# Loads of a kernel's opening in another order, and one modulation tile moved from VectorE to TensorE

## The reference

```python
def ada_mods(cvec, w, b):
    m = jax.nn.silu(cvec) @ w + b
    return [t[:, None, :] for t in jnp.split(m, 6, axis=-1)]

def post_norm_layer(x, mods, mixer, channel, ln):
    sh1, sc1, g1, sh2, sc2, g2 = mods
    y, state = mixer(x * (1 + sc1) + sh1)
    x = layer_norm(ALPHA * x + g1 * y, ln[0], ln[1])
    x = layer_norm(ALPHA * x + g2 * channel(x * (1 + sc2) + sh2), ln[2], ln[3])
    return x, state
```

## Time and profile before

| | |
|---|---|
| median of 3 runs | 1607.42 us (1606.74 to 1607.65) |
| the profiled execution | 1608.91 us |
| its span, first to last instruction | 1607.2 us |
| TensorE busy | 1505.2 us, 94% of the span |
| VectorE busy | 1262.9 us, 79% |
| ScalarE busy | 798.8 us, 50% |
| GpSimd busy | 333.4 us, 21% |
| mean granted clock of TensorE | 0.973 |
| mean DMA rate | 218 GB/s |

### The profile page before, as it was taken

The page is one execution under the profiler, slowest core; times in us unless marked ns, Lnnn a source line. Parts: engine busy times, 40 slices in busy tenths (PEclk is TensorE's granted clock), DMA queues, the critical chain, the costliest instruction groups (busy, mean ns, idle before and its releaser), DMA issues. The chain is left out here.

```text
span 1607.2 us, 23836 instructions
## 1 busy us (share of the span) xinstructions
PE 1505.2 (94%) x8787; PEld 1362.6 (85%) x8787; DVE 1262.9 (79%) x1667; ACT 798.8 (50%) x1066; POOL 333.4 (21%) x410
## 2 busy tenths in 40 slices
PE   5999999799999998999999797899999999999996
PEld 1768876599999998997776695899999999999994
DVE  6868798688887977987778644788888888888884
ACT  1222222533332226545677325567677776777763
POOL 1201003600101103004995043001011010110104
PEclk9999999899999999999998899999999999999998
DMA  9534344256566632323221036689999999999960
GB/s 384 196 104 162 128 144 144 104 209 222 212 225 229 229 117 88 131 106 118 80 82 63 0 141 255 252 301 370 369 377 356 348 365 364 382 351 347 364 245 40
DMA packets 50151, 349.68 MB, mean 218 GB/s; under 512 B 6016, under 2 KB 6416, under 8 KB 22432
## 3 DMA queue, kind: packets, MB, share of 16 engines
q1 hardware_dynamic: 31392, 278.88, 45.0%
q0 software_dynamic: 18256, 68.30, 12.9%
q10 hardware_dynamic: 432, 1.57, 0.2%
HBM read 335.22 MB, written 13.50 MB: 217 GB/s over the span
## 5 line engine op out<-in xcount | busy, mean ns | idle before, releaser
L1992 DVE TENSOR_TENSOR arena_r<-arena,arena_r 128x2816 fp32r<-128x2816 f32 x132 | 406.1, 3090 | 54.4 <-ACT arena_r L1117 53.0
L2862 PE MATMUL ps<-arena_r,uT_r 128*128 128x352 f32 (+1 forms) x1188 | 367.1, 309 | 0.0
L1117 ACT ACTIVATE arena_r<-arena 128x2816 fp32r<-128x2816 f32 x132 | 337.4, 2556 | 54.2 <-PE ps L2862 52.1
L2862 PE MATMUL ps<-arena_r,zT_r 128*128 128x352 f32 x1408 | 346.7, 327 | 5.7 <-DVE uT_r L2090 4.3
L2498 PE MATMUL ps<-sqT_r,arena_r 128*128 128x384 f32 x963 | 260.2, 342 | 7.5 <-DVE uT_r L1658 7.5
L2862 PEld LDWEIGHTS ps<-arena_r,zT_r 128*128 128x128 f32 x1408 | 247.3, 189 | 6.1 <-DVE arena_r L1992 6.1
L2862 PEld LDWEIGHTS ps<-arena_r,uT_r 128*128 128x128 f32 x1188 | 224.9, 189 | 0.0
L2498 PEld LDWEIGHTS ps<-sqT_r,arena_r 128*128 128x128 f32 x963 | 178.1, 190 | 8.5 <-issue 8.5
L2862 PE MATMUL ps<-arena_r,spare_r 128*128 128x256 f32 x968 | 177.8, 285 | 4.0 <-DVE arena_r L1992 4.0
L2498 PE MATMUL ps<-arena_r,arena_r 128*128 128x384 f32 x848 | 160.7, 342 | 8.3 <-DVE arena_r L1862 5.7
L2498 PEld LDWEIGHTS ps<-arena_r,arena_r 128*128 128x128 f32 x848 | 149.9, 191 | 11.2 <-DVE arena_r L1862 6.5
(11 more groups left out here) (459 smaller groups left out, 2481.6 us busy)
## 6 DMA issues: line engine op xcount, KB each, us to landing
arena<-in_w_moe SPq DMA_DIRECT2D x132, 1408.0 KB, 7.6
arena<-in_w_up SPq DMA_DIRECT2D x22, 1024.0 KB, 4.9
zT<-in_w_adav POOLq DMA_DIRECT2D x32, 512.0 KB, 4.8
arena<-in_w_xbc SPq DMA_DIRECT2D x12, 1024.0 KB, 4.9
arena<-in_w_down SPq DMA_DIRECT2D x8, 1408.0 KB, 6.4
spare<-in_w_adav POOLq DMA_DIRECT2D x20, 512.0 KB, 5.2
sqT<-in_w_adav POOLq DMA_DIRECT2D x16, 512.0 KB, 3.9
arena<-in_w_z SPq DMA_DIRECT2D x8, 1024.0 KB, 4.8
```

Of the source, the lines that this page charges most:

```text
L1117: nc.scalar.activation(whi[s % PAIRS], slot(s % MRING), ACT.Copy) \
L1992: V.tensor_tensor(wlo[s % PAIRS], slot(s % MRING), whi[s % PAIRS].bitcast(F32), ALU.subtract) \
L2862: m = M.matmul(out, a, b, start=first and n == 0, stop=last and n == 2)
```

## The change

`ADA_PE` goes from 4 to 5 and `ADA_FIRST` from 4 to 3: one of the eight first tiles moves from VectorE, and from GpSimd's queue, to TensorE and SyncE's queue. The fifth tile uses slot 0 again, so its load waits for the first tile's matmuls. All later tiles move one slot on in the ring.

On SyncE's queue the order becomes `cvec`, tile 0, `consts`, tile 1, `pvec`, tiles 2, 3 and 4, `xT`, `masks`. The condition now counts on `x_in`: ScalarE's first SiLU waits for the condition alone, and `modulate` for the condition, `xT` and the masks. `ada_turn` waits for the constants and column vectors at its first call.

On VectorE `ada_first`, `modulations` and `modulate` come ahead of the mask cast, `sel2` and the identity cast.

```diff
--- before.py
+++ after.py
@@ -67,7 +67,7 @@
 NPV = _at
 
 
-ADA, ADA_PE, ADA_FIRST = 24, 4, 4
+ADA, ADA_PE, ADA_FIRST = 24, 5, 3
 ADA_UP, ADA_TURN = 32, (0, 2, 3, 1)
 ADA_REST = 2 * (ADA - ADA_PE - ADA_FIRST)
 
@@ -468,10 +468,7 @@
 
         @block.sync
         def _(sp):
-            sp.dma_start(cons[:, :], i["consts"]).then_inc(S("consts_in"), 16)
-            sp.dma_start(pvec[:, :], i["pvec"]).then_inc(S("consts_in"), 16)
-            sp.dma_start(masks, i["masks"]).then_inc(S("consts_in"), 16)
-            sp.dma_start(cvec, i["cvec"]).then_inc(S("consts_in"), 16)
+            sp.dma_start(cvec, i["cvec"]).then_inc(S("x_in"), 16)
 
             def load(name, width, t, k):
                 g = FIRST[name] + t
@@ -486,6 +483,10 @@
                     if first + t >= RING:
                         sp.wait_ge(*tile_done(first + t - RING))
                     load(name, width, t, t)
+                    if (name, t) == ("ada0a", 0):
+                        sp.dma_start(cons[:, :], i["consts"]).then_inc(S("consts_in"), 16)
+                    elif (name, t) == ("ada0a", 1):
+                        sp.dma_start(pvec[:, :], i["pvec"]).then_inc(S("consts_in"), 16)
                 loops = (n - head) // RING
                 if loops:
                     with sp.Fori(0, loops) as it:
@@ -500,7 +501,9 @@
             for name, *_ in STAGES:
                 stream(name)
                 if name == "ada0a":
+                    sp.wait_ge(S("x_in"), 16)
                     sp.dma_start(xT[:, :, :], i["xT"]).then_inc(S("x_in"), 16)
+                    sp.dma_start(masks, i["masks"]).then_inc(S("x_in"), 16)
 
             def load_expert(e, s):
                 sp.dma_start(slot(s % MRING), i["w_moe"][e, s] if isinstance(e, int) else
@@ -758,7 +761,7 @@
                                              bias=mod(layer, 3 * half, b, grp), scale=mod(layer, 3 * half + 1, b, grp))
                 k.then_inc(S("u_ready"), 1)
 
-            act.wait_ge(S("consts_in"), 64)
+            act.wait_ge(S("x_in"), 16)
             nc.scalar.activation(cact, cvec, ACT.Silu).then_inc(S("cact_ready"), 1)
             act.wait_ge(S("cond_in"), 16)
             nc.scalar.activation(crow[0], crow[0], ACT.Silu).then_inc(S("cond_ready"), 1)
@@ -1374,19 +1377,18 @@
             step(V.memset(onesf[:, :], 1.0))
             step(V.memset(epsc, EPS))
             step(V.memset(onesm[:, :], 1.0 / D))
-            v.wait_ge(S("consts_in"), 64)
+            v.wait_ge(S("cond_ready"), 1)
+            ada_first()
+            v.wait_ge(S("consts_in"), 32)
+            v.wait_ge(S("tr_mm"), ADA_PE)
+            modulations(0, 0, 2 * KB, 1)
+            v.wait_ge(S("x_in"), 48)
+            modulate(0, 0, 0)
             step(V.tensor_copy(maskb16[:, :, :], masks))
             twins = ident.rearrange("p (e w h) -> p e w h", e=2, w=2)
             step(V.tensor_tensor(sel2[:, :].rearrange("p (e h) -> p e h", e=2), twins[:, :, 0, :], twins[:, :, 1, :],
                                  ALU.add))
             step.done(V.tensor_copy(identb16[:, :], ident), S("b16_ready"), 1)
-
-            v.wait_ge(S("cond_ready"), 1)
-            ada_first()
-            v.wait_ge(S("tr_mm"), ADA_PE)
-            modulations(0, 0, 2 * KB, 1)
-            v.wait_ge(S("x_in"), 16)
-            modulate(0, 0, 0)
             step(V.memset(vaug[:, :, :, HD:VA], 1.0))
             ada_rest(4)
 
@@ -2187,6 +2189,8 @@
             def ada_turn(t):
 
                 pe.wait_ge(S("cact_ready"), t + 2)
+                if t == 0:
+                    pe.wait_ge(S("consts_in"), 32)
                 for j in range(2):
                     m = M.transpose(ps[:, 5, 4 * t + 2 * j:4 * t + 2 * j + 2], adarow[:, t % 2, j * P:(j + 1) * P],
                                     ident[0:2, 0:2])
```

## The result

The changed kernel took 1612.24 us (median of 20 runs, 1607.02 to 1617.49), the kernel before 1607.82 (20 runs beside it, 1604.17 to 1612.65). The ratio is 1.0023 with a 95% interval of 1.0013 to 1.0033: slower by 3.7 us (2.1 to 5.3). The forecast was 1608.5, its range ended at 1610.8. The profiled execution took 1610.3 us with a span of 1608.6.

A forecast was written before the change was run, and what follows sets the result against it. The prediction took the opening's transfers to set VectorE's modulation start at 34.88 us, delaying everything behind one for one. Two tiles behind one landing gave +1.1, all else nothing: 1607.42 + 1.1 = 1608.5 us, range 1606.2 to 1610.8.

The forecast's parts named there:

- Three small operations moved behind the modulation: VectorE after modulating: mask cast, sel2 and identity cast, 0.75 us together, hidden in 1.95 us of idle time.
- TensorE nothing, as it runs full to 98 on loads that are there: If the streamed row landed earlier, the three operations would cost VectorE 0.75 us and TensorE nothing.
- Two tiles' work stands behind one landing: Opening, TensorE: tiles 3 and 4 both follow tile 3's landing, so modulation starts at 36.0 against 34.88, +1.1 us.
- 4.2, as the fourth tile now ... to 26.9: SyncE's queue, opening: tile 3's load takes 4.2 us beside GpSimd's small loads and lands at 26.9.
- Rival B: Opening, TensorE: tile 2 starts slow, modulation starts at 37.3, +2.4 us, 1609.8; chance 0.14.
- The rule that the prediction weighed here: TensorE's clock: a matmul loop waiting for a DMA between tiles can start every tile cold; 1.6 us for the first.
- Rival A: Opening: loads bind, not TensorE; modulation starts with the masks at 34.0 to 34.8, 1606.5 to 1607.3; chance 0.20.
- Rival C: Opening, TensorE: tile 2 stays slow throughout, 7.24 us, modulation starts at 39.3, +4.4 us, 1611.8; chance 0.07.
- small rows on SyncE's queue are paid by their number: While GpSimd's queue moves 8 KB rows, SyncE's loads pay by 128 rows, not bytes; column vectors 2.6 to 3.3 us.
- The wait on tile 0's matmuls: SyncE's queue: tile 4's load waits for slot 0 until 11.7, needed only at 26.9, so it costs nothing.
- Ring positions: Later tiles move one slot on; first MoE load issued 8.3 us sooner, its first user starts at 978.50, no gain.
- rival D: Expert stage begins early through the earlier first MoE load, up to 8.3 us, 1600.2; chance 0.03.

The follow-up runs named there:

- experiment 4: Kernel before with five first tiles on TensorE and three on VectorE, nothing else changed; ratio 1.0011 to the kernel before.
- experiment 2: Kernel before with only mask cast, sel2 and identity cast moved behind the modulation; 1615.71 us, ratio 1.0044 to the kernel before.
- experiment 1: Changed kernel with sel2 and identity cast moved ahead of VectorE's wait, mask cast left behind; 1609.04 us, ratio 1.0006 to the kernel before.
- experiment 6: Changed kernel with GpSimd's multiplication of xT held until the identity cast is done; 1610.36 us, ratio 1.0005 to the kernel before.
- experiment 12: Kernel of experiment 7 with the multiplication of xT by ALPHA on ScalarE instead of GpSimd; 1608.56 us, ratio 0.9999 to the kernel before.
- experiment 3: Changed kernel with the first tiles split four and four again, new load order and moved operations kept; ratio 1.0022 to the kernel before.
- experiment 7: Kernel before with condition, constants, column vectors loaded first, masks behind toka's loads, sel2 and identity cast early, mask cast later; 1606.58 us, ratio 0.9988.
- 11: Kernel of experiment 7 unchanged, timed a second time; ratio 0.9992 to the kernel before.
- 8: Kernel of experiment 7 with GpSimd's seven small loads issued behind its first two streamed tiles; ratio 0.9993 to the kernel before.

## Why the prediction was wrong

**The step that failed** is "*Three small operations moved behind the modulation* ... 0.75 us together ... VectorE has 1.95 us of idle time there ... They are hidden." They took 8.2 us. The price came from a place where GpSimd's timeline has nothing, and was carried to one where it has an instruction of 8 us. The sign of it stood in the prediction's own rows: the earlier trace rows give the first streamed reduction 5.33 us, give sixteen of the same form 1225 ns each. Something took 4.1 us from VectorE at exactly the place that the operations were moved to.

The length of the block alone is not the cost, as experiment 4 shows. In each of the 13 traces with GpSimd's multiplication, VectorE's first held instruction gets in 6.11 to 6.17 us after GpSimd's start. In before that is the reduction, which ends 14.3 us behind M, with 1.95 us of idle time and 4.1 of block in front of it. In the changed kernel sel2 takes that opening, the cast behind it is held once more, until GpSimd is through (53.00), and the first reduction ends 16.5 us behind M. Those 2.2 us put the next streamed loads later, and the second of them beside SyncE's 1 MB load: 2.5 more. In the four traces with the operations in this place it is issued between 1.0 us behind and 0.2 us ahead of SyncE's and is used 6.5 to 7.4 us after its issue; in the ten others it is issued at least 0.8 us ahead and used after 3.9 to 4.1. That second half is read from the traces; no run changed it alone, nor moved sel2 or the cast without the other. The end of the quoted step fails too: a delay would cost "TensorE nothing, as it runs full to 98 on loads that are there". TensorE also needs VectorE's chain, for the bank that ScalarE frees and for the queries at Q, and had 2.9 and 1.6 us of slack there against a delay of 4.6.

Experiments 2 (makes the loss), 1 and 6 (take it away, in two ways) and 12 (GpSimd's part gone, the reduction at 1.23) show the cause. The term: 0 forecast, measured +2.9 to +4.9 at Q (64.66 to 66.04 less 61.13 to 61.81). In timed runs experiments 1 and 6 are 1.7 to 2.5 thousandths below the changed kernel's two ratios, 2.7 to 4.0 us; taken pair by pair, the intervals still touch in three of four. Added to the forecast, the changed kernel's 3.65 would have given 1612.2, where 1612.24 was measured; that agreement is partly luck, since the opening lost more than its 1.1.

The Trainium skill ("SBUF — State Buffer", section "🔬 SBUF: two separate sides") has the rule: VectorE and GpSimd share a pair of ports as an exclusive lock, the loser "fully blocks", and besides the two-port modes it takes VectorE's instructions with two SBUF inputs against a GpSimd instruction that reads SBUF. sel2 and the reduction have two such inputs, the multiplication reads SBUF. The trace agrees: 6.14 instead of 0.23, 5.33 instead of 1.22. The cast has one input and took 1.70 instead of 0.23; whether it ran in a two-port mode no row says outright. 128 more columns cost a cast 0.06 us (0.29 against 0.23), and 64 more cost a two-input sum as much, which fits a doubled rate. The section has the pair taken for the whole instruction, and there the trace differs: VectorE got in 6.1 us after the start of an instruction of 8.0 (last section). The prediction didn't weigh this rule, though it speaks against the change.

**The opening: mechanism right, size short.** "Two tiles' work stands behind one landing" is what the trace shows; M grew by 1.2 to 3.2 us (37.95 and 38.12 against the three values of before; +1.9 between the means), forecast +1.1 with +3.0 as the upper end. Tile 3 is the mis-sized landing: "4.2, as the fourth tile now ... to 26.9". In the changed kernel tile 2 hid when it landed, but experiment 1, the same order, waited for it until 28.77, and experiment 3 until 28.71. 28.77 less 23.71 (tile 2's start there) is 5.1 us and not 4.2. That is half of the 1.9 us by which the landing was missed (26.9 forecast); the other half is in the loads ahead of it, as tile 2 came at 23.71 there and not at 22.7. A tile 3 at 28.8 is the forecast's own upper end, which gave M 37.9. Experiments 1 and 6, in which only the opening's loss is left, are slower by 0.6 and 0.5 thousandths, 0.8 to 1.0 us, which their intervals don't tell from no change.

**Rival B** (tile 2 starts slow) came true in its picture: 5.26 us in the changed kernel, 5.09 in experiment 6, but 3.61 and 3.62 in experiments 1 and 3, with gaps before it of 2.29, 2.35, 2.48 and 2.38 us. It hardly counted: experiment 1's M is 0.2 us earlier than the changed kernel's, as tile 3 landed at 28.8 in any case. The rule that the prediction weighed here (the Trainium skill, "TensorE: Matmul & The Clock Gate", section "HAM oscillation — how this bites in real kernels") holds for tile 1, behind gaps of 2.80 to 4.41 us, in all five traces with the new order of loads (5.14 to 5.30 us), and for tile 2, behind 2.29 to 2.48, in three of them. **Rival A** is answered: TensorE, not the masks, released VectorE (masks 36.1, transposes 37.06). **Rival C** didn't occur.

**Loads.** That small rows on SyncE's queue are paid by their number once GpSimd's queue runs was right: the column vectors 2.8 us in the new place, and in experiment 7 the tiles started 2.4 us sooner once the masks and the condition no longer stood between. The wait on tile 0's matmuls held the queue until 12.1 (11.7 forecast) and cost nothing that shows: tile 3 landed at 28.77 with it (experiment 1) and at 28.71 without (experiment 3, where no modulation tile waits).

**Ring positions, rival D.** The first MoE load was issued at 953.02 in the changed kernel; by the delay of 4.5 us that the trace has there, that is 8.3 us sooner than before (956.87 + 4.45 - 953.02), and its first user started at 982.97, 4.47 later than the earlier trace rows. No gain, as forecast.

**What stays open.** At Q the two traces of the changed kernel are 6.0 us behind the three of before on the mean (103.56 less 97.54), the timed runs 3.7 and 4.8. Behind Q executions differ by steps (last section), and the profiled changed kernel ended 1.4 us behind the profiled kernel before, where Q says 6.7. Whether one or two us of the loss are given back later on, or only the few traces differ, the runs don't settle. Experiment 2's Q is 5.6 us behind that mean, within the 4.8 to 9.5 of its timed runs.

## What to carry to other kernels

Before a small instruction is moved "into idle time", look at what the other engines do in that stretch, and compare the instruction that stands there now with its own kind elsewhere: one row of 5.33 us among sixteen of 1.22 is a queue for something, and the moved work will stand in it. Then ask when the work behind it gets through, which loads that work sets off and what they will meet, and how much slack the engine behind it has. Four us less on VectorE gained nothing (experiment 12), and 4.6 more cost 3 to 4. When a load's landing sets the answer, take a second trace of the kernel before: here it moved by 1.9 us, more than the effect forecast.

## What the runs showed of the hardware that was not expected

**VectorE is let in before GpSimd's instruction ends.** Taking its own 0.23 us off, sel2 got in at 45.12 + 6.14 - 0.23 = 51.03 in the changed kernel, 6.17 us after the multiplication's start at 44.86, in experiment 2 6.17 (start 44.01) too; the reduction in experiment 6 at 47.40 + 6.20 - 1.23 = 52.37, 6.11 after 46.26, in the kernel before 6.11 after 41.80 (43.81 + 5.33 - 1.23), and in experiment 4, where it asked 0.11 us behind GpSimd's start, 6.12. GpSimd's row lasts 8.0. Both times are 0.06 us longer in just the five traces in which the mask cast runs when GpSimd starts (6.17 and 8.05, against 6.11 and 7.99). The identity cast behind sel2 then waits again, until 53.00, just past GpSimd's end at 52.91, while the reduction behind the first one takes its usual 1.23. So the block isn't simply the whole of GpSimd's row; why it opens at 6.1 wasn't tried, and GpSimd's spans are rough.

**Executions of one kernel differ in steps.** In a dense stage of TensorE two kinds of execution occur. Groups of instructions from 340 to 480 us, the changed kernel, then the kernel before:

```profile
L2502 PE MATMUL ps<-uT_r,arena_r 128*128 128x384 f32 x270 | 90.5, 335 | 0.0
```

```profile
L2498 PE MATMUL ps<-uT_r,arena_r 128*128 128x384 f32 x265 | 89.7, 339 | 0.0
```

The same 140 us hold 270 of them in the one and 265 in the other. The whole stage takes 186.0 us in the changed kernel (from 314.50) and 189.4 in the first trace of before (from 307.26), so a lag of 7.2 us shrinks to 3.9. It isn't an edit's doing: both traces of the changed kernel and experiments 2, 4, 11 and 12 are of the first kind, the three traces of before and experiments 1, 3, 6, 7 and 8 of the other, and 7 and 11 are the same kernel. Where it comes from is open. Runs of the kernel before spread over 8 us (1604 to 1612).

**One load, two landings.** The fourth modulation tile of the kernel before landed at 29.66, 31.48 and 31.54 us in three executions, with the same issues ahead of it. Whether the chip or the single execution makes it, the runs don't separate.
